# First expert table for 224 of 256 tokens, the other 32 by gathered rows; weight ring with 1 MB slots

## What is computed

```python
def peer(xn, w_pq, sub_k1, sub_k2, expert_u, expert_v):
    q = (xn @ w_pq).reshape(B, S, 8, 2, 128)
    s1, s2 = q[..., 0, :] . sub_k1, q[..., 1, :] . sub_k2      # 128 keys each
    v1, i1 = top_k(s1, 16); v2, i2 = top_k(s2, 16)
    cand = v1[..., :, None] + v2[..., None, :]                # 256 pairs a head
    vs, ci = top_k(cand, 16)
    eidx = i1[ci // 16] * 128 + i2[ci % 16]                   # 128 experts a token
    gates = softmax(vs)
    act = gelu(einsum('tkd,td->tk', expert_u[eidx], xn))
    return einsum('tk,tkd->td', act * gates, expert_v[eidx])
```

## Time and profile before

| | us |
|---|---|
| median of 3 runs (lowest to highest) | 3247.19 (3246.25 to 3251.39) |
| profiled execution | 3245.9 |
| its span, first to last instruction | 3244.2 |
| PE busy | 3119.7 |
| DVE busy | 1828.6 |
| ACT busy | 1343.4 |
| POOL busy | 113.0 |
| HBM read / written, MB | 588.64 / 37.77 |

### The profile page before, as it was taken

One profiled execution on the slowest core, in us unless ns is written; L12 is line 12 of the kernel. 1 busy time (PEld: TensorE's weight loads), 2 busy tenths in 40 slices (PEclk: granted clock), 3 DMA queues, 4 the chain that ended last, 5 costly groups with the idle time before them and its releaser, 6 DMA issues. The chain is left out here.

```text
span 3244.2 us, 37837 instructions
## 1 busy us (share of the span) xinstructions
PE 3119.7 (96%) x15669; PEld 2665.5 (82%) x15669; DVE 1828.6 (56%) x2189; ACT 1343.4 (41%) x1371; POOL 113.0 (3%) x250
## 2 busy tenths in 40 slices
PE   8997599999999999999999999999999999999998
PEld 7996477888887888978888889888988888888876
DVE  4445355444444445554558878888755555555554
ACT  4333444343433444453443344334444444444443
POOL 1002100000000002220000000000000000000000
PEclk9997699999999999999999999999999999999999
DMA  8552045555554444526455556566675666666652
GB/s 281 182 195 74 0 158 179 181 189 198 181 187 174 183 182 151 168 82 259 169 192 205 205 221 234 208 221 224 230 266 211 249 244 244 249 238 233 231 195 89
DMA packets 200557, 629.47 MB, mean 194 GB/s; under 512 B 6793, under 2 KB 82601, under 8 KB 164576
## 3 DMA queue, kind: packets, MB, share of 16 engines
q1 hardware_dynamic: 195056, 607.34, 52.3%
q10 hardware_dynamic: 4528, 17.89, 1.6%
q0 software_dynamic: 832, 2.25, 0.3%
HBM read 588.64 MB, written 37.77 MB: 193 GB/s over the span
## 5 line engine op out<-in xcount | busy, mean ns | idle before, releaser
L180 DVE TENSOR_TENSOR weights_lo<-weights,weights_hi 128x2048 fp32r<-128x2048 f32 (+4 forms) x540 | 1190.4, 2205 | 1101.7 <-ACT weights_hi L173 1101.0
L173 ACT ACTIVATE weights_hi<-weights 128x2048 fp32r<-128x2048 f32 (+4 forms) x540 | 997.4, 1847 | 1678.4 <-PE banks L429 1163.2
L2129 PE MATMUL banks<-peer_features,weights_hi 128*128 128x512 f32 x2304 | 810.1, 396 | 1.9 <-DVE weights_lo L180 1.9
L427 PE MATMUL banks<-weights_hi,features_hi 128*128 128x512 f32 (+3 forms) x1728 | 654.3, 379 | 13.9 <-DVE weights_lo L180 13.9
L429 PE MATMUL banks<-weights_hi,features_lo 128*128 128x512 f32 (+3 forms) x1728 | 651.6, 377 | 0.0
L428 PE MATMUL banks<-weights_lo,features_hi 128*128 128x512 f32 (+3 forms) x1728 | 651.5, 377 | 0.0
L2131 PE MATMUL banks<-peer_features,weights_lo 128*128 128x256 f32 x2304 | 645.8, 280 | 0.0
L2129 PEld LDWEIGHTS banks<-peer_features,weights_hi 128*128 128x128 f32 x2304 | 433.4, 188 | 99.4 <-DVE weights_lo L180 2.3
L2131 PEld LDWEIGHTS banks<-peer_features,weights_lo 128*128 128x128 f32 x2304 | 436.5, 189 | 0.0
L427 PE MATMUL banks<-weights_hi,applied_hi 128*128 128x512 f32 x1024 | 399.0, 390 | 2.4 <-DVE peer_scores L2269 2.4
L428 PE MATMUL banks<-weights_lo,applied_hi 128*128 128x512 f32 x1024 | 399.0, 390 | 0.0
(11 more groups left out here) (356 smaller groups left out, 1934.8 us busy)
## 6 DMA issues: line engine op xcount, KB each, us to landing
weights<-in_expert_u SPq DMA_DIRECT2D x64, 2048.0 KB, 7.9
weights<-in_expert_v SPq DMA_DIRECT2D x64, 2048.0 KB, 7.8
weights<-in_w_ffn_gate SPq DMA_DIRECT2D x22, 2048.0 KB, 7.8
weights<-in_w_ffn_up SPq DMA_DIRECT2D x22, 2048.0 KB, 7.9
weights<-in_w_ffn_down SPq DMA_DIRECT2D x22, 2048.0 KB, 7.7
weights<-in_w_in SPq DMA_DIRECT2D x24, 1800.0 KB, 7.1
weights<-in_w_out SPq DMA_DIRECT2D x16, 2048.0 KB, 8.2
weights<-in_w_in SPq DMA_DIRECT2D x12, 1408.0 KB, 6.3
```

The lines of the kernel that those rows point to most:

```text
L173: act.activation(self.piece(self.hi, half, stream), self.raw(j, stream)[:, half * k:half * k + k], ACT.Copy)\
L180: dve.tensor_tensor(self.piece(self.lo, half, stream), self.raw(j, stream)[:, half * k:half * k + k], self.piece(self.hi, half, stream).bi ...
L427: pe.matmul(out, xh, wh, start=first, stop=False)
L2129: pe.matmul(self.bank(n % 3), wh[:, k, :], F[:, k, :, :].rearrange("p h t -> p (h t)"), start=(k == 0), stop=False)
```

## The change

In the expert stage:

- The first table is multiplied for tokens 32 to 255 only: L2129 has 448 columns and L2131 has 224. The query product keeps its widths.
- For tokens 0 to 31 the chosen rows are fetched from a second copy of the table in its original layout (`expert_rows`, 8 KB per row). 32 indirect DMAs on POOL's queue fetch 128 rows each (1 MB; four rows of each of the 32 tokens, the token in the partition), into three buffers. DVE multiplies each with the scaled token and sums (`tensor_tensor_reduce`, 128 x 2048) at steps 34 + 8c // 3, c = 0 to 31. ACT applies the Gelu to the sums, DVE multiplies them into the gates, and the scores of these tokens in the dense table are 1.
- The one-hots of these 32 tokens come last, in steps 126 to 129; the others' stay in steps 58 to 69 and 110 to 125. Of each four `tensor_scalar` two are replaced by Square and Relu on ACT (not in the last four steps).
- The multiplication with rstd moves from each tile's departure to one DVE instruction per group of 8, over 128 x 1792, just before the Gelu.
- The loads of scores and gates are issued some steps earlier.

In all stages: the ring has four slots of 1 MB, a fill is two DMAs of 1 MB, each waiting for the low half four pieces back, and four pieces instead of eight are fetched for the next stage. `mla` gets tensors of its own in place of the slots' upper halves.

```diff
 class Ring:
     SLOTS = 4
-    WORDS = 4096
     PIECE = 2048
...
-        self.buf = nc.alloc_sbuf_tensor("weights", [P, self.SLOTS, self.WORDS], F32)
+        self.buf = nc.alloc_sbuf_tensor("weights", [P, self.SLOTS, self.PIECE], F32)
...
-        if wait:
-            sp.wait_ge(self.lo_ready, i * 8 + 2 * (fills + j - 3))
-        sp.dma_start(self.raw(j, stream), stream.source(i, j)).then_inc(self.ready[j], 16)
+        k = stream.view[0] // 2
+        for half in range(2):
+            if wait:
+                sp.wait_ge(self.lo_ready, i * 8 + (2 * (fills + j) + half - 3))
+            sp.dma_start(self.raw(j, half, stream), stream.source(i, j)[:, half * k:half * k + k])\
+                .then_inc(self.ready[(2 * j + half) % self.SLOTS], 16)
+
+    def ahead(self, sp, stream, fills):
+
+        for j in range(2):
+            self.fill(sp, stream, 0, j, fills)
 
     def rest(self, sp, stream, following):
 
+        for j in range(2, 4):
+            self.fill(sp, stream, 0, j, self.fills)
...
-            after = self.fills + 4 * stream.rounds
-            for j in range(4):
-                self.fill(sp, following, 0, j, after)
+            self.ahead(sp, following, self.fills + 4 * stream.rounds)
...
-        SC, RET, TURN, HOT = 18, (22, 74), (55, 107), (58, 110)
+        SC, RET, TURN = 18, (22, 74), (55, 107, 119)
+        ROWS, BUFS = 32, 3
+        HOT = [(58 + i, 0, ROWS // 8 + i) for i in range(16 - ROWS // 8)] + [(110 + i, 1, i) for i in range(16)]\
+            + [(126 + i, 0, i) for i in range(ROWS // 8)]
+        SUM = [34 + 8 * c // 3 for c in range(ROWS)]
+        DOTS = SUM[-1] + 1
...
+                    if t == 0:
+                        for quarter in range(4):
+                            k = slice(part * 32 + quarter * 8, part * 32 + quarter * 8 + 8)
+                            last = dve.scalar_tensor_tensor(out=pick[quarter * 32:quarter * 32 + 32, part * 8:part * 8 + 8],
+                                                            in0=eg[0:32, 0, k], scalar=float(NKEYS), in1=eg[0:32, 1, k],
+                                                            op0=ALU.mult, op1=ALU.add)
+                        last.then_inc(listed, 1)
...
+                    for c in range(ROWS):
+                        if c % 8 == 0:
+                            pool.wait_ge(listed, c // 8 + 1)
+                        if c >= BUFS:
+                            pool.wait_ge(row_summed, c - BUFS + 1)
+                        else:
+                            pool.wait_ge(xg_made, 1)
+                        pool.indirect_dma_start(out=rows[:, c % BUFS, :], out_offset=None, in_=rows_d,
+                                                in_offset=bass.IndirectOffsetOnAxis(ap=pick[:, c:c + 1], axis=0))\
+                            .then_inc(gathered[c % BUFS], 16)
...
-                            pe.matmul(self.bank(n % 3), wh[:, k, :], F[:, k, :, :].rearrange("p h t -> p (h t)"),
-                                      start=(k == 0), stop=False)
-                            last = pe.matmul(self.bank(n % 3, T), wl[:, k, :], F[:, k, 0, :], start=False, stop=(k == KD - 1))
+                            lo = 0 if n < U0 else ROWS
+                            pe.matmul(self.bank(n % 3, 2 * (T - lo)), wh[:, k, :], F[:, k, :, lo:T], start=(k == 0), stop=False)
+                            last = pe.matmul(self.bank(n % 3, T - lo), wl[:, k, :], F[:, k, 0, lo:T], start=False, stop=(k == KD - 1))
...
+                    def hot_act(g, gi):
+                        if gi >= 4:
+                            act.wait_ge(gated, gi - 3)
+                        h = hot[g % 4 // 2][:, g % 2]
+                        for c in by_act(gi // 2):
+                            last = act.activation(h[:, 1, c, :], iof[:, :], ACT.Square, scale=-1.0,
+                                                  bias=egT[:, 0, 4 * g + c:4 * g + c + 1])
+                        ch(last)
+                        for c in by_act(gi // 2):
+                            last = act.activation(h[:, 1, c, :], h[:, 1, c, :], ACT.Relu, scale=-16.0,
+                                                  bias=egT[:, 2, 4 * g + c:4 * g + c + 1])
+                        last.then_inc(hots_act, 1)
...
-                        ch(dve.tensor_tensor(rest[:, n % 2, :], ps, rest[:, n % 2, :], ALU.add))
-                        dve.tensor_tensor(S[:, e // 2 % 2, e % 2, :], rest[:, n % 2, :], R[:, :], ALU.mult).then_inc(tile_read, 1)
+                        dve.tensor_tensor(S[:, e // 2 % 2, e % 2, ROWS:T], self.bank(n % 3, DENSE), rest[:, n % 2, 0:DENSE],
+                                          ALU.add).then_inc(tile_read, 1)
...
+                        if s in SUM:
+                            c = SUM.index(s)
+                            dve.wait_ge(gathered[c % BUFS], 16 * (c // BUFS + 1))
+                            last = dve.tensor_tensor_reduce(rows[:, c % BUFS, :], rows[:, c % BUFS, :], xg[:, :], 1.0, 0.0,
+                                                            ALU.mult, ALU.add, dots[:, c:c + 1])
+                            last.then_inc(row_summed, 1)
+                        for g in [g for g in range(NKEYS // 8) if CURVE(g) - 1 == s]:
...
+                            moved = s_in[g % 2][:, :, ROWS:T]
+                            dve.tensor_tensor(moved, moved, R[:, ROWS:T].unsqueeze(1).to_broadcast([P, 8, DENSE]), ALU.mult)\
+                                .then_inc(normed, 1)
```

More of the change, by code:

```diff
@@ L191, in close @@
     def close(self, stream):
-        for j in range(4):
-            self.base[j] += 16 * (stream.rounds - (j >= stream.last))
+        for slot in range(self.SLOTS):
+            self.base[slot] += 8 * (4 * (stream.rounds - 1) + stream.last)
         self.fills += 4 * stream.rounds
@@ L595, in sync @@
             sp.dma_start(self.X[:, :, half(1)], xs[:, :, half(1)]).then_inc(self.tokens[1], 16)
-            for j in range(1, 4):
-                self.ring.fill(sp, first, 0, j, 0, wait=False)
+            self.ring.fill(sp, first, 0, 1, 0, wait=False)
         def tensor(pe, j):
@@ L1443, in mla @@
         Zr = Z[:, :, ROPE_OFF:IN2_COLS]
[L1444 to L1449, removed]
+        wproj = [ring.buf[:, 2 + i, :].rearrange("p (c k n) -> p c k n", c=2, k=2) for i in range(2)]
         tok = lambda t: slice(t * P, (t + 1) * P)
@@ L1573, in _ @@
                     sp.dma_start(wpool, a["w_pool_2"][0].rearrange("g (k p) d -> p g k d", p=P)).then_inc(loaded, 16)
+                    stream.view = views[0].view
+                    for j in range(2, 4):
+                        ring.fill(sp, stream, 0, j, base)
                     stream.view = views[1].view
@@ L1581, in _ @@
                     sp.dma_start(pT[:, :, :], a["p_2"]).then_inc(p_loaded, 16)
[L1582 to L1586, removed]
+                    ring.fill(sp, following, 0, 0, base + 8)
                     sp.wait_ge(loaded, 16)
@@ L1923, in first_sync @@
                 sp.wait_ge(projected, 4)
-                for j in range(2, 4):
-                    ring.fill(sp, following, 0, j, ring.fills)
+                ring.fill(sp, following, 0, 1, ring.fills)
                 sp.wait_ge(projected_read, 4)
@@ L1983, in peer @@
             S = tmp("peer_scores", [P, 2, 2, T])
+            with ExitStack() as c2:
+                early = lambda n, s: c2.enter_context(nc.sbuf_tensor(n, s, F32))
+                chose, choseT = early("row_choice", [P, 4, P]), early("row_choice_turned", [P, 3, ROWS])
             a_hi, a_lo = tmp("applied_hi", [P, 2, 2, T], F32R), tmp("applied_lo", [P, 2, 2, T], F32R)
@@ L2013, in peer @@
             piece_done = lambda n: 2 * ring.fills + n + 3
-            hot_step = lambda s: [(t, s - HOT[t]) for t in range(NT) if 0 <= s - HOT[t] < P // 8]
+            hot_step = lambda s: [(t, r, n) for n, (at_step, t, r) in enumerate(HOT) if at_step == s]
+            late = lambda n: n >= len(HOT) - ROWS // 8
+            by_act = lambda n: () if late(n) else (2, 3)
             def retrieval(dve, ch, t):
@@ L2079, in retrieval @@
                 tail(PARTS - 1)
+                if t == 0:
+                    ch(dve.tensor_copy(chose[0:ROWS, 0:3, :], eg[0:ROWS, 0:3, :]))
                 dve.sem_inc(chosen, 1)
@@ L2085, in _ @@
                 def _(sp):
-                    for f in range(4, FILLS):
+                    for f in range(2, FILLS):
                         stream.view = stream.fill_view(f)
                         ring.fill(sp, stream, f // 4, f % 4, ring.fills)
-                        pair = f - 13
+                        pair = f - 11
                         if 0 <= pair < NKEYS // 2:
@@ L2307, in _ @@
+                        for t, r, place_in_order in hot_step(s):
+                            if place_in_order == 0 or (t == 1 and r == 0) or (late(place_in_order) and r == 0):
+                                dve.wait_ge(choice_read, 3 if late(place_in_order) else t + 1)
                             for g in (2 * r, 2 * r + 1):
```

(2 more changed lines are left out.)

153 lines of the change are left out of this document (107 added, 46 removed).

## The result

| | before | after |
|---|---|---|
| median, us (lowest to highest, 4 runs each) | 3246.72 (3246.22 to 3251.39) | 3210.82 (3208.86 to 3213.80) |
| profiled execution, us | 3245.9 | 3212.7 |
| span, us | 3244.2 | 3211.0 |

The ratio is 0.9887, 95% interval 0.987 to 0.9904: 36 us faster. 3206 had been forecast.

What follows compares the result with a forecast made beforehand. PE, busy 96% of the span, was taken as the bound. Terms −82 + 3 + 34 + 3 + 2 = −40 us from the profiled 3245.9 gave 3206 us; forecast band 3190 to 3225, whole range 3170 to 3255.

Steps and rivals of the forecast that it cites:

- Narrower products: First table's matmuls on PE: 96 fewer columns per pair, 40 ns each, −81.9 us; +3 for a floor near 0.11 us.
- Sums in retrieval steps: Steps 34 to 55 and 74 to 106: DVE's low half comes late, PE waits; 21 x 1.6 = +34 us.
- Each sum pays anew: Retrieval steps: DVE's lead of 1.08 us, shrunk to 0.44, does not grow between sums, so every sum stalls PE.
- Sums in other steps: One-hot steps: DVE needs 7.2 us against a pace of 6.7, with a larger lead and not every step: 0.
- Half the one-hots on ACT: One-hot steps: eight activations of 0.265 us, +2.1 us a step, hidden by ACT's idle time: 0.
- Gathers: POOL queue, 32 of 1 MB: DMA takes 4.3 (bound 4.9) of 5 us per tile, just enough: 0.
- Ring: 1 MB weight slots: 16 us for landing against a median of 13.1: 0, with +3 for restarts at stage borders.
- small work: Rstd multiply 0; row list, scaled tokens, curve and turned weights in light steps, Gelu's ACT table load: taken as +2.
- Rival A: Expert stage: sums are hidden and PE keeps its pace, 3170 us; chance 0.10.
- B: Rival: gathers' descriptors on POOL delay DVE, +25 us beside retrieval, 3231 us; chance 0.12.
- C: Rival: fp32r matmul under 256 columns not paced at one column per cycle, up to about 3710 us; chance 0.07.
- D: Rival: ring starves, gathers or late fills make PE wait for weights; 3264 at 6.5 us per gather; chance 0.10.

Runs made afterwards that it cites:

- The thirds: Changed kernel with each row's sum cut into three pieces spread evenly over steps 34 to 116: 3204.26 us.
- the placed pieces: Spread kernel of sums in three pieces, the pieces placed by DVE's load of each single step: 3180.04 us, ratio to before 0.9784.

## Why the prediction was right, and where it was off

3206 had been forecast and 3211 came out, and the mechanism was the one forecast: a shorter pair on PE, partly paid back in retrieval steps where DVE is late with the low half. That the total is so near is in part luck, since errors ran against each other: the narrowing brought some 11 us less than its two terms say, the sums cost 3 less, and 3 came from before's slower pace in tiles 26 to 57, which no term had.

- *Narrower products, −82 and a floor of +3.* The pair fell from 347 to 313 ns, 68 us over 2048 pairs in place of 79; with the slower pace of before's tiles 26 to 57 the stretch shows 71.2. The mis-sized term: the floor. Of the forecast 40 ns per pair the wide product gave its 27; the low one gave 7 of its 13, because the floor that had been seen in the earlier trace rows ("something near 0.11 us") lies at about 0.109 between load starts. The floor was taken at +3 with +27 as its bound; it is 6 ns x 2048 = 12 us. The Trainium skill ("TensorE: Matmul & The Clock Gate", LDWEIGHTS (loading the stationary operand)) says that a weight load takes its columns divided by 1.2 ns; for 128 columns that is 107 ns, and the 107 to 110 measured agree.
- *Sums in retrieval steps, +34.* Measured 31.4, in 20 waits where 21 were forecast; a step with a sum takes 6.96 us where 6.9 was worked out. Right in mechanism and place. "Each sum pays anew" holds for whole sums in 20 of 22 cases (at step 55 one cost 0.2 us, at 106 nothing). The thirds show that cutting a sum hardly helps, and the placed pieces show that the load of the single step counts. That the short lead is why nothing can be carried over is argued, not tried: no kernel here has a third pair of half-buffers.
- *Sums in other steps, 0.* Right: 6.80 us with and without.
- *Half the one-hots on ACT, 0.* Right for the time, but for less of a reason than given: each lasts 0.39 us on ACT (0.34 from start to start), not 0.265, and DVE would have coped with all of them.
- *Gathers, 0.* Right: the stretch is 707.86 us with them and 707.85 without.
- *Ring, 0, and +3 at borders; small work, +2.* The ring alone is within 0.2% of before. Second table +1.2 and end +0.7 in the profiled execution; the two long tiles of the curve and the last turn (7.44 and 7.28 in place of 6.80) are the +1.1 of the small work.
- *Rival A, no stall*, was what the kernel without sums does (3177) and nearly what better places for the sums reach (3180). *B* falls, since DVE isn't the one that is held: L184 takes 2291 ns beside 32 gathers, as it did before. The Trainium skill's rule ("SBUF — State Buffer", Who interferes with whom) has a DVE instruction with two SBUF inputs contend with a GpSimd instruction that reads SBUF. The trace agrees on POOL's side alone: 24 of 32 gather instructions ended 0.81 us after the low half that they began in. *C* falls: at 224 columns the product is at the floor, not at four cycles per column. *D* falls: the share is 0.79, and a 1 MB weight piece lands in 6.3 us. The Trainium skill's 6.15 us per MB for GpSimd ("DMA: Bandwidth & Descriptors", Bandwidth) isn't what these gathers took of the 16 engines' time: over this stretch their queue shows

```profile
q0 software_dynamic: 4608, 33.56, 11.1%
```

that is 740 us x 0.111 / 33.56 = 2.4 us per MB.

## What to carry to other kernels

When the bounding engine is made faster, work out anew, step by step, what the next engine has to do within one of the shorter steps; here 68 to 71 us of gain shrank to 40 by work that would have cost 8 to 11 at the old pace. Work added to an engine that is idle on average goes where its single steps have room: cutting it into even pieces was worth 5 us of the stretch, cutting and placing them 29. Before a matmul that alternates with others is narrowed, look at the distance of weight loads: at that distance (0.109 us here) taking 32 more columns off brought nothing.

## What the runs showed of the hardware

- Alternating fp32r products reload the weights for each matmul, and their loads started 0.107 to 0.110 us apart around the low product, at 224 and at 192 columns alike; a product of 384 to 512 columns takes its columns at 2.4 GHz and 17 to 19 ns more. All at a granted clock of 1.00.
- Thirty-two indirect DMAs of 1 MB each beside a DVE busy for 82% of the stretch changed no duration of DVE's low halves, and without the sums their removal left the stretch as it was (707.86 and 707.85 us). The other way round POOL was held: its instruction for a gather takes 0.94 to 1.15 us beside no low half, and ends 0.81 us after the end of the low half (2.29 us) inside which it begins.
- The stretch ahead of the expert stage, the same code in thirteen traces, took 1559.3 to 1567.8 us; the granted clock of its first 400 us differs too, 0.88 in the shortest and 0.86 to 0.88 in the others. What sets it was not tried.
